# Two float32r parts in place of three bf16 parts where expert outputs are combined

## What is computed

```python
def swiglu(x, wg, wu, wd):
    return (jax.nn.silu(x @ wg) * (x @ wu)) @ wd

top_w = jnp.take_along_axis(scores, top_idx, axis=-1)
top_w = top_w / top_w.sum(-1, keepdims=True) * ROUTED_SCALE
...
contrib = yb[dest] * w_sorted[:, None]          # expert output times the token's weight
y = jax.ops.segment_sum(contrib, tok_sorted, num_segments=N)
x = layer_norm(DEEPNORM_ALPHA * x + y + swiglu(x, ws_gate, ws_up, ws_down), g, b)
```

## Time and profile before

| | |
|---|---|
| plain runs | 1267.7 us median of 3 (1267.0 to 1270.15) |
| profiled execution, its own time | 1272.96 us |
| profiled execution, its span | 1271.2 us |
| granted TensorE clock, mean | 0.982 of full |
| busy in the span | PE 1210.3 us (95%), PEld 555.0 (44%), DVE 426.7 (34%), ACT 335.5 (26%), POOL 9.5 (1%) |
| loads in the span | 450.15 MB read from HBM, of them 64 x (4096 + 2048) KB of expert weights |
| hardware DMA queue | 84.2% of 16 engines' span |

### The profile page before, as it was taken

One profiled execution on the slowest core, in us unless ns is written; L12 is line 12 of the kernel. 1 busy time (PEld: TensorE's weight loads), 2 busy tenths in 40 slices (PEclk: granted clock), 3 DMA queues, 4 the chain that ended last, 5 costly groups with the idle time before them and its releaser, 6 DMA issues.

```text
span 1271.2 us, 18674 instructions
## 1 busy us (share of the span) xinstructions
PE 1210.3 (95%) x8032; PEld 555.0 (44%) x8032; DVE 426.7 (34%) x1198; ACT 335.5 (26%) x637; POOL 9.5 (1%) x20
## 2 busy tenths in 40 slices
PE   7998899999999999999799898999999999999993
PEld 6763443433343334333286544433433343334330
DVE  0343722333333323332332535232333233323334
ACT  0041222223222322232211411232223222322220
POOL 0000000000000000000010000000000000000000
PEclk9999989999999999999899998999999999999996
DMA  9692369999999999999737914899999999999980
GB/s 381 249 378 115 104 276 426 428 430 432 429 431 424 428 432 432 428 428 429 299 116 307 382 36 166 323 432 429 422 429 432 433 428 426 429 429 428 430 351 35
DMA packets 26721, 452.56 MB, mean 356 GB/s; under 512 B 2944, under 2 KB 3072, under 8 KB 5504
## 3 DMA queue, kind: packets, MB, share of 16 engines
q1 hardware_dynamic: 26624, 451.21, 84.2%
HBM read 450.15 MB, written 1.05 MB: 355 GB/s over the span
## 4 chain that ended last, share of the span: by engine, by line
PE 90%; DVE 4%; DMA 2%; issue 2%; ACT 1%; POOL 0%; SPq 0%; DVEq 0%
PE bank L574 35%; PE bank L600 18%; PE bank L495 8%; PE bank L520 7%; PE bank L660 4%; PE bank L728 3%; PE bank L668 2%; PE bank L586 2%; DMA slots<-in_dense 2%; PE bank L544 2%; PE bank L628 2%; PE bank L689 1%; PE bank L679 1%; PE bank L634 1%; PE bank L507 1%
## 5 line engine op out<-in xcount | busy, mean ns | idle before, releaser
L600 PE MATMUL bank<-slots,scratch 128*32 128x512 f32 x2048 | 233.0, 595 | 2.3 <-issue 2.3
L574 PE MATMUL bank<-slots,xT 128*64 128x512 f32 x1024 | 226.1, 594 | 1.0 <-ACT xT L888 1.0
L574 PE MATMUL bank<-slots,scratch 128*64 128x512 f32 x1024 | 226.0, 594 | 0.0
L1149 DVE SCALAR_TENSOR_TENSOR scratch<-bank,small,scratch 128x512 f32<-128x512 f32 x128 | 96.1, 751 | 248.7 <-ACT scratch L888 248.7
L888 ACT ACTIVATE scratch<-bank,small 128x512 bf16<-128x512 f32 x128 | 88.0, 688 | 159.0 <-PE bank L600 159.0
L888 ACT ACTIVATE scratch<-bank 128x512 f32<-128x512 f32 (+2 forms) x122 | 67.2, 562 | 237.2 <-PE bank L495 76.8
L495 PEld LDWEIGHTS bank<-scratch 128*128 128x128 bf16 x1536 | 107.7, 147 | 50.4 <-issue 49.7
L574 PEld LDWEIGHTS bank<-slots,xT 128*64 128x64 f32 x1024 | 69.3, 137 | 130.6 <-issue 129.3
L574 PEld LDWEIGHTS bank<-slots,scratch 128*64 128x64 f32 x1024 | 69.2, 137 | 129.4 <-issue 129.4
L495 PE MATMUL bank<-scratch 128*128 128x128 bf16 x1536 | 117.1, 227 | 0.3
L600 PEld LDWEIGHTS bank<-slots,scratch 128*32 128x32 f32 x2048 | 60.7, 109 | 121.1 <-issue 117.1
(11 more groups left out here) (125 smaller groups left out, 708.2 us busy)
## 6 DMA issues: line engine op xcount, KB each, us to landing
slots<-in_w_gu SPq DMA_DIRECT2D x64, 4096.0 KB, 22.7
slots<-in_w_dn SPq DMA_DIRECT2D x64, 2048.0 KB, 21.0
slots<-in_dense SPq DMA_DIRECT2D x32, 1024.0 KB, 11.1
r<-in_pool_mat SPq DMA_DIRECT2D x2, 1024.0 KB, 14.1
r<-in_ln_g SPq DMA_DIRECT2D x4, 512.0 KB, 4.0
r<-in_ln_b SPq DMA_DIRECT2D x4, 512.0 KB, 6.5
slots<-in_shared_dn SPq DMA_DIRECT2D x2, 1024.0 KB, 4.8
scratch<-in_memt SPq DMA_DIRECT2D x2, 512.0 KB, 5.8
```

The source lines that it names most:

```text
L574: m = pe.matmul(H[64 * a:64 * a + 64, :], xg[B % 2][:, k, j, a, :], GU[g][:, a, :, k, :], start=k == 0, stop=k == KD - 1)
L600: m = pe.matmul(Y[half][r0:r0 + 32, :], hT[:, kc * P + 64 * a + 32 * t:kc * P + 64 * a + 32 * t + 32], DN[g][:, a, kc, half * 512:(half + ...
L1149: dve.scalar_tensor_tensor(yres[:, half * 512:(half + 1) * 512], Y[half][:, :], wslot[:, b:b + 1], ysp[:, 0, half * 512:(half + 1) * 512], ...
```

## The change

The weighted expert outputs are kept in two float32r parts instead of three bf16 parts. Part 0 is Y x wslot written as float32r by ScalarE, part 1 is Y x wslot - part 0, written as float32r by VectorE, straight into `ysp[:, 1]`. The f32 residual `yres`, ScalarE's two copies for part 1 and VectorE's two subtractions for part 2 are gone, and with them the semaphores `res_rd` and `mid_rd`; `lo_rd` is now raised by the residual instruction. `selT` becomes float32r (4 bytes) too. `combine` issues 8 matmuls in place of 12.

The work buffer is laid out anew for this: `scratch` becomes `low`, `high`, and `yparts` of type float32r, which shares its place with the first part of `high`; `hT` and `w3` move into the room of `xres`, tile 0. The order of instructions on every engine is otherwise as before, and SyncE's program is the same.

```diff
+        low = sb("low", [P, YS_AT])
+        with nc.sbuf_tensor("yparts", [P, 2 * D + 2 * P], F32R) as yparts:
+            pass
+        high = sb("high", [P, SCRATCH - YS_AT])
+        ysp = yparts[:, 0:2 * D].rearrange("p (s d) -> p s d", s=2)
+        selT = yparts[:, 2 * D:].rearrange("p (b s) -> p b s", b=2)
...
             def combine(ps, n, b):
                 pe.wait_ge(ps.lo_rd, 2 * n + 2)
                 for half in range(2):
-                    for s in range(3):
+                    for s in range(2):
                         for t in range(NT):
                             m = pe.matmul(acc[2 * t + half][:, :], selT[64 * t:64 * t + 64, b, :],
                                           ysp[64 * t:64 * t + 64, s, half * 512:(half + 1) * 512],
...
                         if not first:
-                            pe.wait_ge(ps.res_rd, 2 * n - 1 + half)
+                            pe.wait_ge(ps.lo_rd, 2 * n - 1 + half)
...
                         copy(ysp[:, 0, half * 512:(half + 1) * 512], Y[half][:, :], scale=wslot[:, b:b + 1])\
                             .then_inc(ps.hi_rd, 1)
-                    for half in range(2):
-                        act.wait_ge(ps.res_rd, 2 * n + half + 1)
-                        copy(ysp[:, 1, half * 512:(half + 1) * 512], yres[:, half * 512:(half + 1) * 512])\
-                            .then_inc(ps.mid_rd, 1)
...
                         dve.wait_ge(ps.hi_rd, 2 * n + half + 1)
-                        dve.scalar_tensor_tensor(yres[:, half * 512:(half + 1) * 512], Y[half][:, :], wslot[:, b:b + 1],
-                                                 ysp[:, 0, half * 512:(half + 1) * 512], ALU.mult, ALU.subtract)\
-                            .then_inc(ps.res_rd, 1)
+                        dve.scalar_tensor_tensor(ysp[:, 1, half * 512:(half + 1) * 512], Y[half][:, :], wslot[:, b:b + 1],
+                                                 ysp[:, 0, half * 512:(half + 1) * 512].bitcast(F32), ALU.mult, ALU.subtract)\
+                            .then_inc(ps.lo_rd, 1)
                     if not last:
                         take_selT(n + 1, 1 - b)
-                    for half in range(2):
-                        dve.wait_ge(ps.mid_rd, 2 * n + half + 1)
-                        dve.tensor_tensor(ysp[:, 2, half * 512:(half + 1) * 512], yres[:, half * 512:(half + 1) * 512],
-                                          ysp[:, 1, half * 512:(half + 1) * 512], ALU.subtract).then_inc(ps.lo_rd, 1)
```

More of the change, by code:

```diff
@@ L20 @@
 BF16 = mybir.dt.bfloat16
+F32R = mybir.dt.float32r
 I32 = mybir.dt.int32
@@ L42 @@
 SMALL_W = KD * E + E + 2 * HD + 2
-SCRATCH = 9920
+SCRATCH = 9856
+YS_AT = 6144
 BLOCKS = PAIRS // 2
@@ L166, in build @@
         power = sb("power", [P, 1])
-        scratch = sb("scratch", [P, SCRATCH])
+        low = sb("low", [P, YS_AT])
[4 more added lines that the diff above has]
+        selT = yparts[:, 2 * D:].rearrange("p (b s) -> p b s", b=2)
         off = [0]
         def part(n, dt=F32):
-            v = scratch[:, off[0]:off[0] + n]
+            v = low[:, off[0]:off[0] + n] if off[0] < YS_AT else high[:, off[0] - YS_AT:off[0] - YS_AT + n]
             off[0] += n
+            assert off[0] <= YS_AT or off[0] - n >= YS_AT
             assert off[0] <= SCRATCH, off[0]
@@ L198, in build @@
         xres = part(NT * D).rearrange("p (t d) -> p t d", t=NT)
-        yres = xres[:, 0, :]
-        off[0] -= D
+        off[0] -= NT * D
+        hT = part(2 * F)
+        w3 = part(NT * E * 3 // 2, BF16).rearrange("p (t e s) -> p t e s", t=NT, s=3)
+        off[0] += D - 2 * F - NT * E * 3 // 2
         xg_odd = part(KD * 2 * P)
-        ysp = part(3 * D // 2, BF16).rearrange("p (s d) -> p s d", s=3)
+        off[0] += 2 * D + 2 * P
         hh = part(2 * F).rearrange("p (t n) -> p t n", t=NT)
-        hT = part(2 * F)
         sg = part(2 * F).rearrange("p (t n) -> p t n", t=NT)
         sel = part(2 * NT * P // 2, BF16).rearrange("p (b t c) -> p b t c", b=2, t=NT)
-        selT = part(2 * P // 2, BF16).rearrange("p (b s) -> p b s", b=2)
         pos = part(NT * E)
-        w3 = part(NT * E * 3 // 2, BF16).rearrange("p (t e s) -> p t e s", t=NT, s=3)
         off[0] = NT * 3 * D // 2 + D + KD * 2 * P
@@ L225, in build @@
         top = part(NT * 8)
-        assert off[0] <= NT * 3 * D // 2 + D + KD * 2 * P + 3 * D // 2
+        assert off[0] <= YS_AT + 2 * D
         counts_i = sb("counts_i", [P, 1], I32)
@@ L313, in __init__ @@
                 self.hi_rd = sem(f"{tag}_hi_rd")
-                self.res_rd = sem(f"{tag}_res_rd")
-                self.mid_rd = sem(f"{tag}_mid_rd")
                 self.lo_rd = sem(f"{tag}_lo_rd")
@@ L918, in body @@
                             .then_inc(ps.hi_rd, 1)
-                    for half in range(2):
-                        act.wait_ge(ps.res_rd, 2 * n + half + 1)
-                        copy(ysp[:, 1, half * 512:(half + 1) * 512], yres[:, half * 512:(half + 1) * 512])\
-                            .then_inc(ps.mid_rd, 1)
                 pairs_of_pass(base, body)
             def skipped(n):
-                for s_, k in ((more.g_sb, 2), (more.silu_rd, 1), (more.hi_rd, 2), (more.mid_rd, 2)):
+                for s_, k in ((more.g_sb, 2), (more.silu_rd, 1), (more.hi_rd, 2)):
                     act.sem_inc(s_, n * k)
@@ L1163, in skipped @@
                 for s_, k in ((more.selT_sb, 1), (more.h_rd, 1), (more.hT_sb, 1),
-                              (more.res_rd, 2), (more.lo_rd, 2)):
+                              (more.lo_rd, 2)):
                     dve.sem_inc(s_, n * k)
```

## The result

| | before | changed |
|---|---|---|
| median | 1270.15 us (9 runs, 1267.0 to 1273.1 without one outlier of 3165) | 1262.11 us (9 runs, 1258.92 to 1265.26) |
| profiled execution | 1272.96 us, span 1271.2 | 1263.89 us, span 1262.1 |

The ratio is **0.9942, 95% interval 0.9926 to 0.9959**: 0.6% faster, which is the size that was forecast (7.8 us; 1260 us in a range of 1248 to 1266). The two medians are 8.0 us apart; the ratio leaves the outlier out and makes it 7.4 us. The sum hid errors that went opposite ways: transfers bound later than forecast, and the stretch between the layers, put at nothing, grew.

A forecast was written before the change was run, and what follows sets the result against it. TensorE was taken to bound the kernel, weights landing barely ahead. Pair 31's lead, pair 30's combine, and the last combine's earlier start and shorter length gave 3.6 us in layer 0 and 4.2 in layer 1, together 7.8: 1260 us, range 1248 to 1266.

The forecast's parts named there:

- TensorE sets the end, with almost nothing left behind it: Expert stages: TensorE sets the pace; pair 31's weights land only 1.38 us (layer 1: 1.99) before they are needed.
- I take one pass: Combine: a float32r step costs one pass, 0.217 us, so the combine falls from 1.40 to 0.97, a gain of 0.43.
- I take hidden: Combine: the longer weight loads, 186 ns, hide behind the step before, 0.217 us, and cost nothing.
- the third rival: Combine gains nothing, as weight loads show or a step has other overhead: 1261.5, 1265 or 1285 us; chance 0.12.
- ends near pair ... 21: Expert stages: the weights' lead of 20.0 us at pair 4 shrinks by 1.08 a pair and ends near pair 21.
- 20 to 25 us: Profile after: a new wait of TensorE for gate/up loads, some 22 times and 20 to 25 us in all.
- The lead: Pair 31 can start earlier by the time its weights land before use: 1.38 us in layer 0, 1.99 in layer 1.
- 1.38 at the end of each layer: Last combine of each layer: it waits for the second residual alone and starts 1.38 us earlier.
- 0.43 in it: Last combine of each layer: it takes 0.43 us less itself.
- What follows ... only moves along: After each layer's last combine, the 4.10 us before L628 included: the stretch shifts earlier with no change in length.
- Rival 1: Expert weights: transfers are faster without the profiler, giving 1255 us, or 1237.5 if they never bind; chance 0.17.
- Rival 2: Combine: a float32r step costs more than one pass: 1293 us (chance 0.08), or 1404 at full f32 price (0.03).

The follow-up runs named there:

- half_after: The changed kernel with every expert load from pair 3 of each layer on bringing half of its bytes: 1248.36 us, ratio 0.9825.
- half_before: The kernel before with every expert load from pair 3 of each layer on bringing half of its bytes: 1267.85 us, ratio 0.9984.
- one_part: The changed kernel with part 1 left out of the combine, 4 matmuls a pair in place of 8: 1260.9 us, ratio 0.9927.
- split_before: The kernel before with each gate/up load in two halves, the first issued half a product earlier, each with its own semaphore: 1270.03 us, ratio 1.0009.
- hold: The changed kernel with layer 1's second and third dense chunk asked for only after VectorE read layer 0's first sum: 1259.7 us, ratio 0.993.
- bf16_two: The kernel before with its third bf16 part left out of the combine alone, 8 bf16 matmuls: 1265.95 us, ratio 0.9972.
- split_hold: The changed kernel with gate/up loads in two halves and layer 1's second and third dense chunk asked for after the branch: 1252.18 us, ratio 0.9874.

## Why the prediction was right, point by point

- **What bounds the kernel.** "TensorE sets the end, with almost nothing left behind it": shown by half_after against half_before (19.5 us) and one_part (31 us less of TensorE's work for 0.2 us of gain).
- **"I take one pass."** Right in kind: one record a matmul and 0.23 us a step against 0.217.
- **"I take hidden"** for the weight loads. Here a term was mis-sized. The loads are hidden between steps but not at the start, and the combine is 1.12 instead of 0.97: 0.27 us saved a pair instead of 0.43. "186 is less than 217" compared one load with one step, while each step has two loads and the first has none before it to hide behind. It is the third rival's mechanism at less than half of its size (0.15 us a combine in place of 0.37). It cost nearly nothing, since this saving is given back in any case; where transfers don't bind, it costs 64 x 0.15 = 10 us.
- **"ends near pair ... 21", "20 to 25 us" of waits.** Followed from the 0.43. With 0.27 the same working has the lead shrink by 0.92 from 19.2 and end at pair 25; the trace has the first waits at pairs 27 and 26, 11 in all, 9.4 us.
- **The lead.** 1.38 and 1.99 were forecast between pair 0 and pair 31, 3.14 and 1.60 measured. The landings were 0.06 us closer in layer 0, 1.6 us over 28 pairs. That is not another rate: "14.83" is a mean of intervals of 14.6 and a few of about 16, and before, the last of the four long ones fell on pair 31 (landings 561.72 + 30.9 = 592.6 and 608.75, 16.1 apart), where in the changed kernel these two are 552.52 + 36.7 = 589.2 and 603.86, 14.6 apart, with three long ones in the layer. Where a long interval falls moves a layer's end by 1.5 us, and here it fell well.
- **1.38 at the end of each layer**: 16.08 - 14.45 = 1.63 with the combine of pair 30, against 1.77 forecast. In layer 1 the same 1.63 was used up by the clock.
- **"0.43 in it"**, the last combine of each layer: 1.89 to 1.21 and 2.08 to 1.19. More than forecast, as part of it ran at the lower clock before (mean 0.73 in the window above) and none does now. The prediction had no clock in it here either.
- **"What follows ... only moves along"** was the step that failed. The gap at the branch grew by 2.75 us, because the stage ended while loads that had been issued in it still filled the DMA engines. Nor did the prediction have the clock's 1.7 us; it had counted waits, but nothing behind them. Together they took back 4.5 us of the trace's gain.
- **Rival 1** rested on the 5.3 us between profiled and plain time. With 9 runs the median before is 1270.15 and a plain run reaches 1273.1: it was scatter, and most of it stands in the trace: 4.5 us in layer 0's dense stage (174.1 us to the first expert product, 169.6 in half_before and split_before). Faster transfers show in no run. **Rival 2** is excluded by the records.

So what bounds the kernel, before and after, was right, and the total was right in part by luck. In the traces the expert stages with the gap behind them give 5.1 us (2.7 in layer 0, 2.4 in layer 1) where 7.8 were forecast, and only the faster dense stages of this execution bring it to 9.1. The medians, which don't rest on one pair of executions, give 7.4 to 8.0 us with an interval of 5.2 to 9.4, which holds 7.8 and would hold 5.5 as well. Why they lie above the 5.1 is not shown; executions in which the clock doesn't fall, as in hold's trace, would add 1.7.

## What to carry to other kernels

A chain with no transfer in it doesn't say that transfers are far from binding: compare the distance of the landings with that of the issues, and the last load's landing with its use. A saving on the paced engine is worth what is left of that lead, and then asking for data earlier or in smaller pieces is worth more than less work. When a stage ends sooner, look at what was issued in it for the next one and what shares its engines: such loads can be asked for later.

## What the runs showed of the hardware

- A float32r matmul of 64 rows by 512 columns is one record and takes 0.23 us a step with two row groups side by side, against 0.217 in bf16; its 128-column weight load takes 184 ns against 94. The Trainium skill, "FP8 and Floating Point Precision", section "TensorE Precision Notes", has the reduced-precision read without a price; if float32r is that read, the runs give it.
- Behind some of the longer waits for weights TensorE ran at the lower clock: waits of 2.27 and 2.50 (one_part), 2.81 (changed) and 2.86 us (bf16_two) were followed by a product of 8.78 to 8.79 us, one of 2.91 us (hold) by 7.09, and all such waits up to 1.68 us by 7.09. Each of these five long waits falls on one of the long landing intervals of the next point. So the loss of 1.7 us hangs on where such an interval falls, and even then doesn't always come; no run here shows what decides it.
- The expert stream ran at 14.7 to 14.9 us for 6.29 MB, 422 to 427 GB/s, in every kernel with full loads, whatever TensorE did. Every nine or ten intervals (133 to 148 us) one is 0.9 to 1.6 us longer than the usual 14.6 to 14.7; only in layer 0 of split_hold does none stand out. No run here shows its cause.
- With a DMA share of 0.85 to 1.01 behind the start of layer 0's last combine, the first packet of instruction queue q14 came 2.2 to 2.9 us after that start, and with a share of at most 0.53 it came after 0.2 to 0.4 us.
